# A fused transformer kernel: ten modulation blocks placed in the heads, one in the MLP moved by a step, and the last rows shared between VectorE and GpSimd

## The reference

```python
mod = silu(c) @ ada_w + ada_b                       # 6 x 1024 numbers
sh1, sc1, g1, sh2, sc2, g2 = split(mod, 6)
h = rmsnorm(x, norm_mix_w) * (1 + sc1) + sh1
(hq, hf, hi, hg, ..., cu) = split(h @ w_in)
mix = concat([hgrn2_mixer(hq, hf, hi, hg), dsa_mixer(...), conv_module(cu)]) @ w_out
x = x + g1 * mix
h = rmsnorm(x, norm_mlp_w) * (1 + sc2) + sh2
ff = square(relu(h @ mlp_w1)) @ mlp_w2              # 1024 -> 4096 -> 1024
x = x + g2 * ff
return rmsnorm(x, final_norm_w)
```

## Time and profile before

| | |
|---|---|
| median of 3 runs | 1283.53 us (1283.34 to 1284.35) |
| the profiled execution's own time | 1285.01 us |
| its span, first to last instruction | 1283.2 us |
| mean granted clock of TensorE | 0.992 of full speed |
| PE busy | 1257.9 us, 98% |
| PEld busy | 1007.0 us, 78% |
| DVE busy | 692.6 us, 54% |
| ACT busy | 662.8 us, 52% |
| POOL busy | 370.2 us, 29% |

### The profile page before, as it was taken

How to read it: one execution, slowest core, us unless ns; L and a number is a source line. 1 busy time by engine, 2 the same in 40 slices (tenths; PEclk the granted TensorE clock), 3 DMA queues, 4 the chain that set the end, 5 groups by cost and what they waited for, 6 DMA issues and landing times.

```text
span 1283.2 us, 19176 instructions
## 1 busy us (share of the span) xinstructions
PE 1257.9 (98%) x7186; PEld 1007.0 (78%) x7186; DVE 692.6 (54%) x1464; ACT 662.8 (52%) x1261; POOL 370.2 (29%) x189
## 2 busy tenths in 40 slices
PE   9999999999999999899999999999999999999997
PEld 8677777778877777688676888887887888888887
DVE  6656666675565666565798536566763121121224
ACT  6655656666437666625667876752442231231331
POOL 0000000003410000053497774122355354353450
PEclk9999999999999999999999999998999999999998
DMA  5322243442333322252222011124463223233232
GB/s 198 106 66 83 82 143 120 129 134 94 107 97 99 99 83 87 78 175 81 81 83 82 18 50 50 50 83 148 148 197 115 79 94 112 78 115 99 82 99 66
DMA packets 38411, 128.11 MB, mean 100 GB/s; under 512 B 4640, under 2 KB 7584, under 8 KB 38320
## 3 DMA queue, kind: packets, MB, share of 16 engines
q1 hardware_dynamic: 35792, 121.91, 30.1%
q10 hardware_dynamic: 2528, 4.98, 1.1%
HBM read 123.43 MB, written 2.13 MB: 98 GB/s over the span
## 4 chain that ended last, share of the span: by engine, by line
PE 84%; issue 7%; DVE 3%; ACT 2%; DMA 2%; POOL 2%; ACTq 0%; DVEq 0%; POOLq 0%
PE G L834 20%; PE G L836 19%; PE G L835 19%; PE S L946 2%; PE O L1007 2%; PE S L1637 2%; PE T L986 1%; PE S L1173 1%; PE N L867 1%; PE O L1236 1%; PE T L1220 1%; POOL wL L469 1%; DMA w<-weights_dram 1%; POOL tmp L504 1%; PE N L1348 1%
## 5 line engine op out<-in xcount | busy, mean ns | idle before, releaser
L469 POOL TENSOR_TENSOR wL<-w,wH 128x1024 fp32r<-128x1024 f32 x119 | 291.5, 2454 | 852.3 <-ACT wH L1877 852.3
L834 PE MATMUL G<-hi,wH 128*128 128x512 f32 x1208 | 496.0, 411 | 2.0 <-DVE lo L2879 1.1
L836 PE MATMUL G<-hi,wL 128*128 128x512 f32 x1208 | 472.7, 391 | 0.0
L835 PE MATMUL G<-lo,wH 128*128 128x512 f32 x1208 | 472.3, 391 | 0.0
L834 PEld LDWEIGHTS G<-hi,wH 128*128 128x128 f32 x1208 | 227.7, 188 | 62.4 <-issue 14.9
L1877 ACT ACTIVATE wH<-w 128x1024 fp32r<-128x1024 f32 x170 | 179.1, 1054 | 177.7 <-PE G L836 118.5
L835 PEld LDWEIGHTS G<-lo,wH 128*128 128x128 f32 x1208 | 228.3, 189 | 49.2 <-issue 6.2
L836 PEld LDWEIGHTS G<-hi,wL 128*128 128x128 f32 x1208 | 227.7, 189 | 49.8
L917 DVE SCALAR_TENSOR_TENSOR xT<-G,modT,xT 128x512 f32<-128x512 f32 x34 | 25.4, 750 | 123.2 <-PE G L836 123.2
L2348 ACT ACTIVATE tmp<-G 128x512 f32<-128x512 f32 x31 | 18.5, 598 | 119.8 <-PE G L836 116.2
L2371 DVE TENSOR_TENSOR wL<-w,wH 128x1024 fp32r<-128x1024 f32 x51 | 62.3, 1221 | 33.3 <-ACT wH L1877 32.6
(11 more groups left out here) (440 smaller groups left out, 1898.9 us busy)
## 6 DMA issues: line engine op xcount, KB each, us to landing
w<-weights_dram SPq DMA_DIRECT2D x170, 512.0 KB, 3.5
adaw<-ada_dram SPq DMA_DIRECT2D x48, 512.0 KB, 4.0
kd<-c_dram ACTq DMA_DIRECT2D x8, 512.0 KB, 3.3
xT<-x_dram SPq DMA_DIRECT2D x4, 512.0 KB, 8.0
out_dram<-xT SPq DMA_DIRECT2D x8, 256.0 KB, 2.5
scr<-ca_dram SPq DMA_DIRECT2D x2, 512.0 KB, 4.9
kd<-cbias SPq DMA_DIRECT2D x8, 128.0 KB, 3.3
cbias<-ca_dram SPq DMA_DIRECT2D x1, 512.0 KB, 4.9
```

Of the source, the lines that this page charges most:

```text
L469: g.tensor_tensor(wL[:, u.slot], w32[:, u.slot % 2], wH[:, u.slot].bitcast(f32), ALU.subtract).then_inc(w_lo, 1)
L834: mm(home[:, :], whi, H[:, k, :], start=(k == first), stop=False)
L835: mm(home[:, :], whi, L[:, k, :], start=False, stop=False)
L836: last = mm(home[:, :], wlo, H[:, k, :], start=False, stop=(k == final))
```

## The change

The ten ADA_OM blocks move into windows 2 and 3 of the heads: block 0 behind the convolution's centring and blocks 1 and 2 behind the states in window 2; in window 3, block 3 behind the silu of the head before, blocks 4 and 5 behind the convolution's first silu step, 6 and 7 behind joined part 3, 8 behind joined part 6; block 9 stays behind the last head. Even blocks go to the lower half of adaw, odd ones to cbias. SyncE issues their loads between the weight loads. In the MLP's quarter 0 the last ADA_M block goes behind the low part of tile 7. In the last half, TensorE does six products of ones, whose result nobody reads; ScalarE multiplies rows 0 and 1 with the constants of the norm ahead of the last square; the inverse root is spread a second time, into S[0], copied to SBUF by ScalarE, and GpSimd multiplies rows 0 and 1 with it, while VectorE writes rows 2 to 7. The order of the last four stores changes.

```diff
+        end_rows, end_root = kd[:, 0:2, 0:256], kd[:, 2, 0:256]
+        def block_home(b):
+            return flat[:, 0:1024] if b % 2 == 0 else cactb_a
 # SyncE
+            def load_block(b):
+                wait(sp, sem("ada_summed"), ADA_OM + b - 1)
+                sp.dma_start(block_home(b), a["ada"][ADA_OM + b]).then_inc(sem(f"ada_here{b % 2}"), 16)
-            repeated(sp, 4, head)
-            for n in range(5):
-                load_unit(Unit(UOM + n))
+            repeated(sp, 3, head)
+            sp.wait_ge(sem("a_logits"), 80)
+            load_block(0)
+            for j in range(12, 15):
+                load_unit(Unit(UH + j))
             sp.wait_ge(sem("conv_added"), 60)
             load_cactb(cactb)
-            sp.wait_ge(sem("a_logits"), 80)
-            load_ada(Block(ADA_OM, 0))
-            sp.wait_ge(sem("h_diff"), 30 + since("h_diff"))
-            for n in range(1, 8):
-                load_ada(Block(ADA_OM, n))
+            load_unit(Unit(UH + 15))
+            load_unit(Unit(UOM))
+            sp.wait_ge(sem("conv_sqsum"), 1)
+            load_block(1)
+            load_block(2)
+            load_unit(Unit(UOM + 1))
+            load_block(3)
+            load_unit(Unit(UOM + 2))
+            load_block(4)
+            load_block(5)
+            load_unit(Unit(UOM + 3))
+            load_block(6)
+            load_unit(Unit(UOM + 4))
+            for b in range(7, 10):
+                load_block(b)
             for n in range(8):
                 load_unit(Unit(UOM + 5 + n))
-                if 3 <= n <= 6:
-                    load_ada(Block(ADA_OM, n + 5))
+                if n == 3:
+                    sp.wait_ge(sem("h_diff"), 32 + since("h_diff"))
+                    load_ada(Block(ADA_M, 0))
+                    load_ada(Block(ADA_M, 1))
...
+            for k in range(0, KT, 2):
+                store(k, 0, "h32_f", k + 2)
+            store(2, 1, "h32_f", 10)
+            store(4, 1, "h32_f", 12)
+            store(0, 1, "end_rows", 2)
+            store(6, 1, "h32_f", 14)
 # GpSimd, at the end
+            g.wait_ge(sem("end_root"), 1)
+            for k in range(2):
+                g.tensor_tensor(xT[:, k, HALF[1]], end_rows[:, k, :], end_root, ALU.mult).then_inc(sem("end_rows"), 1)
 # half_sums(pe, key, h, constants=0), behind the products of the summed squares
+            for n in range(constants):
+                mm(G[0][:, 0:P], ones[:, :], ones[:, :], start=True, stop=True)
 # half_vector
-                half_rows(dve, key, 1)
+                half_rows(dve, key, 1, range(2, KT))
 # TensorE, at the end
-            half_sums(pe, "f", 1)
+            half_sums(pe, "f", 1, 2)
+            for n in range(4):
+                mm(G[0][:, 0:P], ones[:, :], ones[:, :], start=True, stop=True)
             half_spread(pe, "f", 1)
+            for q in (2, 3):
+                last = mm(S[0][:, q * P:(q + 1) * P], n_root[:, q:q + 1].broadcast_to((P, P)), ident[:, :], start=True, stop=True)
+            last.then_inc(sem("end_spread"), 1)
 # ScalarE, at the end, behind last_squares
+            for k in range(2):
+                s.activation(end_rows[:, k, :], xT[:, k, HALF[1]], ACT.Copy, scale=table[:, gain + k:gain + k + 1])
             half_square(act, "f", 7, 1, sem("x_f"), 24)
             half_scalar(act, "f", 1)
+            act.wait_ge(sem("end_spread"), 1)
+            s.activation(end_root, S[0][:, HALF[1]], ACT.Copy).then_inc(sem("end_root"), 1)
 # VectorE, window(t)
...
                 if t == 2:
                     conv_centre()
+                    blocks(0, 1)
+                if t == 3:
+                    blocks(3, 4)
                 if t == 3:
                     for k in range(2):
                         silu_vector_1(dve, "cv", k, cacc[:, k, :], cv_th[k])
+                    blocks(4, 6)
                 operand(t, 4)
...
                 joined(t, 3)
+                if t == 3:
+                    blocks(6, 8)
...
                 states_of(t)
+                if t == 2:
+                    blocks(1, 3)
...
                 joined(t, 6)
+                if t == 3:
+                    blocks(8, 9)
 # VectorE, behind window 3
-            dve.wait_ge(sem("h_aT"), 28 + since("h_aT"))
-            for b in range(6):
-                ada_block(dve, Block(ADA_OM, b), 48)
+            blocks(9, 10)
             normed_h(3)
 # VectorE, quarter 0 of the MLP
-                    if n < 8 and isinstance(c, int) and c == 0:
-                        ada_block(dve, Block(ADA_M, n))
+                    if n != 7 and isinstance(c, int) and c == 0:
+                        ada_block(dve, Block(ADA_M, min(n, 7)))
```

More of the change, by code:

```diff
@@ L90 @@
 ADA_A, ADA_B, ADA_OB, ADA_OM, ADA_M = 0, 12, 24, 30, 40
-ADA_PER = {"b": (ADA_OB, (0, 1, 1, 1, 1, 2)), "m": (ADA_OM + 6, (0, 0, 1, 1, 1, 1))}
+ADA_PER = {"b": (ADA_OB, (0, 1, 1, 1, 1, 2))}
 ADA_MORE = (0, 2, 4, 6)
@@ L455, in _, with store @@
                 load_unit(Unit(UM + n))
[L456 to L459, removed]
+            def store(k, h, name, count):
+                sp.wait_ge(sem(name), count + since(name))
+                sp.dma_start(out[:, k:k + 2, HALF[h]], xT[:, k:k + 2, HALF[h]]).then_inc(sem("o_stored"), 16)
+            for k in range(0, KT, 2):
[4 more added lines that the diff above has]
+            store(6, 1, "h32_f", 14)
             sp.wait_ge(sem("o_stored"), 16 * KT)
@@ L640, in norm_sums, with half_sums @@
             last.then_inc(sem(f"total_{key}"), 1)
-        def half_sums(pe, key, h):
+        def half_sums(pe, key, h, constants=0):
             tokens = [2 * h, 2 * h + 1]
@@ L928, in add_output, with ada_block @@
                 scaled_low(dve, key, KT - 1)
-        def ada_block(dve, b, fresh=None, copy=cactb):
+        def ada_block(dve, b, fresh=None, copy=cactb, home=None):
+            home, here = (adab[:, b.buffer, :], 0) if home is None else (home, 1)
             if fresh is not None:
@@ L934, in ada_block @@
             dve.wait_ge(sem(f"ada_here{b.buffer}"), b.of_buffer * 16 + 16)
-            v.memset(stat[:, b.buffer, 0, 0:1], 0.0)
-            v.tensor_tensor_reduce(out=adab[:, b.buffer, :], in0=adab[:, b.buffer, :], in1=copy, scale=1.0, scalar=0.0,
+            v.memset(stat[:, b.buffer, here, 0:1], 0.0)
+            v.tensor_tensor_reduce(out=home, in0=home, in1=copy, scale=1.0, scalar=0.0,
                                    op0=ALU.mult, op1=ALU.add, accum_out=modsum[:, b.n:b.n + 1]).then_inc(sem("ada_summed"), 1)
@@ L2359, in _ @@
             last_squares(act, "f", sem("x_f"), 24)
+            table, gain = NORMS["f"][0:2]
+            for k in range(2):
+                s.activation(end_rows[:, k, :], xT[:, k, HALF[1]], ACT.Copy, scale=table[:, gain + k:gain + k + 1])
             half_square(act, "f", 7, 1, sem("x_f"), 24)
             half_scalar(act, "f", 1)
+            act.wait_ge(sem("end_spread"), 1)
+            s.activation(end_root, S[0][:, HALF[1]], ACT.Copy).then_inc(sem("end_root"), 1)
         @block.vector
@@ L2782, in conv_low, with blocks @@
                                     ).then_inc(sem("cv_gated_lo"), 1)
+            def blocks(first, last_):
+                for b in range(first, last_):
+                    ada_block(dve, Block(ADA_OM, b), 48, home=block_home(b))
             def window(t):
```

## The result

| kernel | median | lowest to highest | executions |
|---|---|---|---|
| before, beside it on the same chip | 1283.43 us | 1282.69 to 1284.35 | 6 |
| changed | 1276.74 us | 1273.15 to 1277.15 | 6 |

The ratio is 0.9942, with a 95% interval of 0.9929 to 0.9955. It is the measurement's own estimate and not the quotient of the two medians, which is 0.9948. Three executions further down, one of *mblock* and two of *b5*, ran at a granted clock of 0.65 to 0.75, took 1557 to 1781 us and are left out of every figure. The profiled execution's own time was 1275.75 us beside a span of 1274.0.

The account below looks back on a forecast made before the run. TensorE, busy 98% of the span, was taken as the bound. Stalls 4.2, less 0.2 for blocks in the heads, plus 0.4 for the tail gave 4.4 us off 1283.5: 1279.1 us, main range 1278.2 to 1280.3.

Parts of the forecast that it names:

- The three stalls: TensorE waits at 886.29 (last head's low part), 907.56 (addition of tile 5), 969.95 (eighth MLP tile's low part): 4.2 us back.
- The late load of block 5: Start of window 3: load lands at 843.5 to 844.7, operand starts 2.9 us late; charged 0.2, bounds 0 to 1.2.
- SyncE's queue: Block loads between weight loads delay the fourth output unit's load some 2 us, but nothing waits: cost and gain nothing.
- The tail's 0.4: Behind the last product: 0.4 us gained, chosen between 0.5 if products of ones hold the clock and 0.3 lost otherwise.
- the 0.3 of loss with slow spreads: In the tail, if the clock doesn't hold, the second spread is slow and the third store late: 0.3 us lost.
- The doubt that the prediction drew from the earlier trace: From 872 to 880 the clock was low though TensorE was busy, so narrow filler might not help the tail: 0.3 lost.
- (a): Last head's low part, 886.29: its chain no longer waits for blocks, is ready well before TensorE asks; all 0.57 us returns.
- (c): Eighth MLP tile, 969.95: with the block behind the low part, TensorE gets back 1.1 of 1.22 us.
- The clock changes in the heads: Rival, 0.07: new timing spares one half-clock stretch like 872 to 880, worth 3.4 us; time 1275.7 to 1277.4.
- Window 3 stalls: Rival, 0.13: blocks 5 to 7 meet late loads or splits, TensorE waits for operands; middle price 2 us, 1281.1.
- The large stall stays: Rival, 0.05: another late input takes over the 2.42 us wait at the addition; price 2.6 us, 1281.7.
- A head starves: Rival, 0.06: in window 3 VectorE falls behind, TensorE stalls 3.6 us and its clock falls for 3.4 more; 1286.1.

Follow-up runs that it names:

- mblock: The kernel before with only the last modulation block of the MLP moved behind the last low part; 1282.76 us, ratio 0.9992 against before.
- b5: The changed kernel with block 5 moved behind joined part 3, to block 6, and block 7 behind joined part 6, to block 8; 1276.84 us, ratio 0.9945 against before.
- tail: The kernel before with only the change's edits behind the last product; 1282.98 us, ratio 0.9995 against before.
- consts: The kernel before with the six products of ones only; 1284.26 us, ratio 1.0008 against before.
- poolrows: The kernel before with the second spread and GpSimd's rows only, without the products of ones; 1283.06 us, ratio 0.9995 against before.
- dense_before: The kernel before with the narrow products of a head's output broken into pieces by wider ones; 1282.96 us, ratio 0.9998 against before.
- four: The kernel before with ten blocks rearranged: four in the heads, six behind the last head, none behind the output additions; 1283.03 us, ratio 0.9996 against before.
- delay: The changed kernel with VectorE doing the norm's last step of the last head six times instead of once; 1281.90 us, ratio 0.9984 against before.
- six: The kernel before with the first six blocks moved into the heads, the last four left behind the output additions; 1281.13 us, ratio 0.9983 against before.
- again: The changed kernel measured a second time, with a second profile; 1276.59 us, ratio 0.9942 against before.
- b5_again: The kernel of b5 measured a second time; 1274.96 us, ratio 0.9933 against before.

## Why the prediction was off

**Right.** The three stalls went, for the reasons given. The late load of block 5 and a possible TensorE wait as its outcome were foreseen. SyncE's queue cost nothing. The tail's 0.4 was 0.50 in the profiled pair and 0.37 in the mean, by the mechanism given for the products of ones; the 0.3 of loss with slow spreads was measured as 0.3. The doubt that the prediction drew from the earlier trace rows was not borne out in the tail, where the products of ones went with a full clock in seven traces of seven. The Trainium skill ("TensorE: Matmul & The Clock Gate", section "What's actually happening") has the clock follow how busy TensorE has been of late; the tail agrees with that, and the stretches of low clock at the earlier trace rows, under a busy engine, don't.

**The step that failed** is (a) of the stalls: "All 0.57 comes back." The wait was the right one, its size that of one execution. TensorE was late itself there, held up by 3.1 us of low clock at the earlier trace rows, a row that the prediction used three times and never set beside the stall that begins 6 us later. In the other five traces in which VectorE's work there is that of before, this wait is 2.4 to 4.3 us. With it failed the step behind the sum: "The savings are differences inside the execution, so I take them off the median". They are differences of that execution alone, and as such nearly right: 3.4 measured for 3.15. The prediction's "ready well before TensorE asks" failed with it: the low part is ready only 0.4 us ahead when the clock holds. Where two engines race, what is saved is measured against what the other engine does in a typical execution.

**The same slip at block 5.** The 2.9 us by which the operand was to start late (847.4 - 844.57 is 2.8) were counted from a time that 1.6 us of low clock at 839 had pushed back. Measured without that it is 3.9, and TensorE's wait is 0.57, or 0.8 by starts, for a charge of 0.2. Where the clock falls at 839 there is no wait.

**A second part of the size** is the clock behind a wait. Behind TensorE waits of 2.0 to 4.3 us the granted clock was 0.5 for about 3 to 7 us in *mblock*, *tail*, *consts*, *poolrows*, *dense_before*, *four*, *delay* and *six*. The one in the earlier trace rows, 2.42 at 907.56, had no such sequel, so it isn't a rule for each wait. The same page of the Trainium skill, in "HAM oscillation — how this bites in real kernels", describes waits for transfers, of some 3 to 5 us, after which the next work starts at the low clock. These eight traces agree, four of them with waits below 3 us. Taking the wait away takes this away too.

**The sum, with what was measured.** Stalls at the head and the additions 5.2 for 3.15; (c), the MLP's block, 1.3 for 1.1 (the instructions that before ran from 912 to 1265 us took 1.32 less in the mean of the six traces with the edit, and the same, within 0.03, in the mean of the seven without it); tail 0.4 for 0.4; block 5 a loss of 0 to 0.8 for 0.2. That is 6.1 to 6.9 beside 6.7 and 7.2 in the two measurements. The prediction's main range, 1278.2 to 1280.3, is narrower than its own bounds add up to (1277.8 to 1281.1), but the result lies outside those too.

**The rivals.** "The clock changes in the heads" named the time range that came, 1275.7 to 1277.4, but by another way: not a stretch behind the narrow products that new timing spares, but those behind the waits, and the waits that the former had hidden. "Window 3 stalls" happened in part (0.6 to 0.8 of 2). "The large stall stays" did not happen. "A head starves" needed a second split in the way, and there was none.

## What to carry to other kernels

A wait in one profile is the difference of two arrival times. Before you price its removal, look in the stretch ahead of it for a low granted clock or anything else that made the waiting engine late, and price the wait without it. Engines that race need more than one profile, or one with the disturbance elsewhere; a kernel that differs in another place serves as such. Waits in one chain cover one another: remove one half, and the other grows, so single-part experiments don't add up.

## What the runs showed of the hardware

The low stretches behind the series of 64-column products were there in some executions of one kernel and missing in others (three in *again*, none of the three in the changed kernel's first profile), and cost 1.6 or 3.1 us apiece; the one profile with wider products between them still had one, at 838 us. With six 128-column products of ones in the 1.25 us in which TensorE otherwise idles, the last spread took 0.71 us in seven traces of seven; without them it took 1.2 in five, 1.02 in one and 0.71 in one. How long the clock then stays up isn't fixed: behind the last spread TensorE idles in both, and the granted clock fell near 1273.2 in the changed kernel's profile, 4.7 us after the spread's end, and at 1269.5 in that of *b5_again*, 1.4 us after it. Among the kernel before's first 29 executions a mean granted clock lower by 0.001 went with a time longer by 0.9 us (0.9 and 0.7 in two further sets).
